# A decoder trunk on eight cores: four chunk loads issued by ScalarE, one norm weight moved, new durations in the scheduler's table

## The reference, cut to what matters

```python
def rmsnorm(x, g):
    return x * rsqrt(mean(x * x, -1) + EPS) * g

for layer in range(2):                      # x: (16, 2048, 1024) float32
    xn = rmsnorm(h, mix_norm_g[layer])
    if layer == 0:
        a, xb, gate_b, gate_c = split(xn @ ab_w_in)          # 4 x 512 columns
        a_out = (trailing mean of a over 2/4/8/16 positions - a) @ pool_w * pool_scale
        b_out = gate_b * conv3(gate_c * xb)                  # causal, width 3
        mix = concat(a_out, b_out) @ ab_w_out
    else:
        u, v, q, k, val = split(xn @ cd_w_in)
        c_out = gelu(u) * (W_s layernorm(gelu(v)) + b)       # chunks of 128 positions
        d_out = stick_breaking_attention(q, k, val)          # strictly causal, 8 heads
        mix = concat(c_out, d_out) @ cd_w_out
    h = h + mix
    h = h + square(relu(rmsnorm(h, mlp_norm_g[layer]) @ w1)) @ w2     # 1024 -> 4096 -> 1024
return rmsnorm(h, final_norm_g)
```

## Time and profile before

| | us |
|---|---|
| median of 3 runs | 2603.14 (2600.72 to 2603.9) |
| the profiled execution, its own time | 2602.82 |
| its slowest core, first to last instruction | 2601.3 (core 6); the other seven 2588.6 to 2600.9 |
| TensorE busy on core 6 | 2523.2 (97%) |
| VectorE, ScalarE, GpSimd busy | 1583.2, 1117.3, 658.0 |
| granted TensorE clock, mean | 0.992 on core 6, 0.991 to 0.994 on the others |
| chain that ended last | TensorE 91%, VectorE 3%, transfers 3%, issue 2%, ScalarE 1% |

### The profile page before, as it was taken

How to read it: one execution, slowest core, us unless ns; L and a number is a source line. 1 busy time by engine, 2 the same in 40 slices (tenths; PEclk the granted TensorE clock), 3 DMA queues, 4 the chain that set the end, 5 groups by cost and what they waited for, 6 DMA issues and landing times.

```text
span 2601.3 us, 38509 instructions; the slowest of 8 cores (2588.6 to 2601.3 us)
## 1 busy us (share of the span) xinstructions
PE 2523.2 (97%) x12055; PEld 1108.3 (43%) x12055; DVE 1583.2 (61%) x2344; ACT 1117.3 (43%) x1749; POOL 658.0 (25%) x1088
## 2 busy tenths in 40 slices
PE   6899999999999999999999999999999999999996
PEld 2344444444444444444444444444444444444342
DVE  4761338567586565457577533677666777767554
ACT  3335223464335643174333444345543465345432
POOL 4531111212112253611245211212212122112121
PEclk9999999999999999999999999999999999999998
DMA  9777885745446897887572233433444335435544
GB/s 186 148 139 153 175 183 132 179 98 131 120 124 153 152 181 155 213 264 231 176 210 84 70 104 104 132 102 86 123 121 134 98 90 118 117 97 165 181 146 144
DMA packets 216686, 371.81 MB, mean 143 GB/s; under 512 B 90208, under 2 KB 98016, under 8 KB 216480
## 3 DMA queue, kind: packets, MB, share of 16 engines
q0 software_dynamic: 79664, 238.86, 38.3%
q1 hardware_dynamic: 136240, 129.36, 16.9%
q10 hardware_dynamic: 576, 1.05, 0.1%
HBM read 308.62 MB, written 95.42 MB: 155 GB/s over the span
## 4 chain that ended last, share of the span: by engine, by line
PE 91%; DVE 3%; DMA 3%; issue 2%; ACT 1%; SPq 0%; POOL 0%; DVEq 0%; ACTq 0%; POOLq 0%
PE ps L1400 62%; PE ps L1524 20%; PE ps L1616 6%; DMA h<-xT 2%; PE ps L2283 1%; PE ps L2240 1%; DVE xn L1416 1%; DMA ring<-wcm 1%; DVE Y L1416 1%; SPq L1721 0%; ACT ps L1409 0%; PE ps L2101 0%; DVE h L1413 0%; DVE xn L1413 0%; DVE mix L1413 0%
## 5 line engine op out<-in xcount | busy, mean ns | idle before, releaser
L1400 PE MATMUL ps<-xn,ring 128*128 128x512 bf16 x4960 | 1113.5, 381 | 9.0 <-DVE mix L1413 5.3
L1413 DVE TENSOR_TENSOR h<-ps,h 128x512 f32<-128x512 f32 x816 | 553.3, 688 | 526.2 <-PE ps L1400 295.3
L1400 PEld LDWEIGHTS ps<-xn,ring 128*128 128x128 bf16 x4960 | 473.9, 98 | 578.1 <-issue 20.8
L1409 ACT ACTIVATE ps<-ps 128x512 f32<-128x512 f32 x644 | 375.0, 583 | 703.2 <-PE ps L1400 324.7
L1338 POOL DMA_DIRECT2D ring<-wcm x269 | 143.9, 536 | 779.9 <-PE ps L1400 268.0
L1524 PE MATMUL ps<-hid,ring 128*128 128x512 bf16 x1408 | 327.6, 380 | 2.6 <-DMA ring<-wcm 2.2
L1409 ACT ACTIVATE hid<-ps 128x512 bf16<-128x512 f32 x496 | 294.4, 598 | 37.0 <-ACT ps L1409 1.9
L1338 POOL DMA_DIRECT2D ring<-wsc x308 | 165.9, 539 | 487.7 <-PE ps L1400 189.4
L1409 ACT ACTIVATE xn<-h 128x2048 bf16<-128x2048 f32 (+1 forms) x98 | 154.0, 1591 | 311.9 <-DVE h L1413 291.8
L1400 PE MATMUL ps<-hid,ring 128*128 128x512 bf16 x1280 | 281.0, 380 | 0.0
L1524 PE MATMUL ps<-TT,ring 128*128 128x512 bf16 x1056 | 255.4, 381 | 3.8 <-ACT ps L1409 3.1
(11 more groups left out here) (123 smaller groups left out, 1694.2 us busy)
## 6 DMA issues: line engine op xcount, KB each, us to landing
ring<-wsc POOLq DMA_DIRECT2D x308, 256.0 KB, 3.1
ring<-wblk POOLq DMA_DIRECT2D x188, 256.0 KB, 5.6
ring<-wcm POOLq DMA_DIRECT2D x93, 512.0 KB, 4.0
ring<-wcm POOLq DMA_DIRECT2D x118, 384.0 KB, 4.0
wsc<-ring SPq DMA_DIRECT2D x116, 256.0 KB, 4.2
wcm<-TT SPq DMA_DIRECT2D x64, 256.0 KB, 2.8
oT<-stg SPq DMA_DIRECT2D x56, 256.0 KB, 5.8
wcm<-ring SPq DMA_DIRECT2D x52, 256.0 KB, 4.1
```

Of the source, the lines that this page charges most:

```text
L1400: ins = pe.matmul(out, lhsT=l, rhs=r, start=(i == 0), stop=(i == n - 1), **({"skip_group_check": True} if skip else {}))
L1409: return self.S.op("act", lambda e: e.activation(out=out, in_=in_, func=func, **kw), rd=rd, wr=wr, dur=0.17 + n * 0.00083, aset=aset)
L1413: return self.S.op(eng, lambda e: e.tensor_tensor(out=out, in0=a, in1=b, op=op), rd=rd, wr=wr, dur=dur)
```

## The change

Three kinds of edit. (1) Of the first tile's eight chunks of x, the odd ones are issued by ScalarE, the even ones by SyncE as before. (2) In the last tile the norm weight of chunk 7 is no longer applied by a ScalarE copy; VectorE multiplies h by weight and ms in one instruction. (3) Durations in the scheduler's table become longer: the sums of a norm, Ln and Exp (`act` adds 0.17 + n * 0.00083), the pooled evictions, the convolution, GpSimd's additions, the attention's first matmuls. A margin per operation is added; its two constants equal `MARGIN`, and the boost `PB` that one of them replaces is 0, so both are without effect.

```diff
+RMARG = 0.6
+PMARG = 0.6
...
-                    r = end if e == "pe" else (r if x.tight else r + MARGIN)
+                    r = end if e == "pe" else (r if x.tight else r + x.marg)
...
-                self.S.op("sp", (lambda t, c, src: (lambda e: e.dma_start(out=self.h[s][:, t, c:c + w, :], in_=src)))(t, c, src),
+                q = "act" if s == 0 and p == 0 and t == 0 and c % 2 else "sp"
+                self.S.op(q, (lambda t, c, src: (lambda e: e.dma_start(out=self.h[s][:, t, c:c + w, :], in_=src)))(t, c, src),
...
-            self.tt("dve", xn[:, t, 0:4, :], xn[:, t, 0:4, :], xn[:, t, 4:8, :], ALU.add, tx, tx[0:4], 1.22)
+            self.tt("dve", xn[:, t, 0:4, :], xn[:, t, 0:4, :], xn[:, t, 4:8, :], ALU.add, tx, tx[0:4], 1.29)
...
-            self.act(self.ms[m][:], self.bap(bi), AF.Ln, [self.t_bank[bi], self.t_cf], [self.t_ms[m]], 512, aset="ln",
+            self.act(self.ms[m][:], self.bap(bi), AF.Ln, [self.t_bank[bi], self.t_cf], [self.t_ms[m]], 620, aset="ln",
...
-                            self.tt("dve", h[:, t, c, :], h[:, t, c, :], self.ms[m][:], ALU.mult,
-                                    [th[c], self.t_ms[m]], [th[c]], 0.65)
+                            if c < 7:
+                                self.tt("dve", h[:, t, c, :], h[:, t, c, :], self.ms[m][:], ALU.mult,
+                                        [th[c], self.t_ms[m]], [th[c]], 0.65)
+                            else:
+                                self.stt(h[:, t, c, :], h[:, t, c, :], g, self.ms[m][:], ALU.mult, ALU.mult,
+                                         [th[c], self.t_ms[m], self.t_cf], [th[c]])
...
-                if final is not None:
+                if final is not None and c < 7:
...
-                         [self.t_Y], 0.15 + 1.15 * fw)
+                         [self.t_Y], 0.15 + 1.41 * fw)
...
-                            [td], 0.15 + 1.9 * fw)
+                            [td], 0.15 + 2.0 * fw)
...
-                S.op("pe", fz, rd=rk + [tm[t][4 + a]], wr=zt, dur=0.25, boost=ZB)
+                S.op("pe", fz, rd=rk + [tm[t][4 + a]], wr=zt, dur=0.28, boost=ZB)
```

More of the change, by code:

```diff
@@ L90 @@
     __slots__ = ("eng", "fn", "deps", "dma", "dur", "lat", "nbytes", "idx", "late", "start", "end",
-                 "sig", "chan", "val", "val2", "vc", "waits", "succ", "npend", "ready", "aset", "boost", "tight")
+                 "sig", "chan", "val", "val2", "vc", "waits", "succ", "npend", "ready", "aset", "boost", "tight", "marg")
 SEMLAT = 0.12
@@ L123, in op @@
         o.tight = False
+        o.marg = MARGIN
         o.eng = eng
@@ L1737, in sums @@
         def sums():
-            self.tt("dve", xn[:, t, 0:4, :], xn[:, t, 0:4, :], xn[:, t, 4:8, :], ALU.add, tx, tx[0:4], 1.22)
-            self.tt("dve", xn[:, t, 0:2, :], xn[:, t, 0:2, :], xn[:, t, 2:4, :], ALU.add, tx[0:4], tx[0:2], 0.69)
-            self.tt("dve", xn[:, t, 0, :], xn[:, t, 0, :], xn[:, t, 1, :], ALU.add, tx[0:2], tx[0:1], 0.43)
+            self.tt("dve", xn[:, t, 0:4, :], xn[:, t, 0:4, :], xn[:, t, 4:8, :], ALU.add, tx, tx[0:4], 1.29)
+            self.tt("dve", xn[:, t, 0:2, :], xn[:, t, 0:2, :], xn[:, t, 2:4, :], ALU.add, tx[0:4], tx[0:2], 0.74)
+            self.tt("dve", xn[:, t, 0, :], xn[:, t, 0, :], xn[:, t, 1, :], ALU.add, tx[0:2], tx[0:1], 0.52)
         def boosted(f, x):
@@ L1754, in rstd @@
                 o.boost = RB
+                o.marg = RMARG
         def rstd1():
@@ L1765, in rstd1 @@
             st["m"] = m
-            self.act(self.ms[m][:], self.bap(bi), AF.Ln, [self.t_bank[bi], self.t_cf], [self.t_ms[m]], 512, aset="ln",
+            self.act(self.ms[m][:], self.bap(bi), AF.Ln, [self.t_bank[bi], self.t_cf], [self.t_ms[m]], 620, aset="ln",
                      scale=1.0 / D, bias=self.cf[:, 60:61])
-            self.act(self.ms[m][:], self.ms[m][:], AF.Exp, [self.t_ms[m]], [self.t_ms[m]], 512, aset="ln", scale=-0.5)
+            self.act(self.ms[m][:], self.ms[m][:], AF.Exp, [self.t_ms[m]], [self.t_ms[m]], 555, aset="ln", scale=-0.5)
         def apply(c0, c1):
@@ L1831, in f @@
                     self.mms(self.bap(bi), [(self.cb[:, 128 + g * 128:256 + g * 128], pb[:, c:c + 512])],
-                             [self.t_cb, self.t_pb], [self.t_bank[bi]], 0.25).boost = PB
-                    self.act(mx[:, t, g, :], self.bap(bi), AF.Copy, [self.t_bank[bi], self.t_cf], [tm[t][g]], 512,
+                             [self.t_cb, self.t_pb], [self.t_bank[bi]], 0.25).marg = PMARG
+                    self.act(mx[:, t, g, :], self.bap(bi), AF.Copy, [self.t_bank[bi], self.t_cf], [tm[t][g]], 620,
                              scale=cf[:, 40 + g:41 + g])
@@ L1861, in f @@
                 b = cf[:, 56 + i:57 + i]
-                self.act(Y[:, 0:W], PR[:, 2:2 + W], AF.Identity, [self.t_PR, self.t_cf], [self.t_Y], W, scale=w2, bias=b)
+                self.act(Y[:, 0:W], PR[:, 2:2 + W], AF.Identity, [self.t_PR, self.t_cf], [self.t_Y], W * 1.26, scale=w2, bias=b)
                 self.stt(Y[:, 0:W], PR[:, 1:1 + W], w1, Y[:, 0:W], ALU.mult, ALU.add, [self.t_PR, self.t_Y, self.t_cf],
-                         [self.t_Y], 0.15 + 1.15 * fw)
+                         [self.t_Y], 0.15 + 1.41 * fw)
                 self.stt(Y[:, 0:W], PR[:, 0:W], w0, Y[:, 0:W], ALU.mult, ALU.add, [self.t_PR, self.t_Y, self.t_cf],
-                         [self.t_Y], 0.15 + 1.15 * fw)
+                         [self.t_Y], 0.15 + 1.41 * fw)
                 if more:
```

## The result

The changed kernel takes 2610.76 us (median of 11 runs, 2606.52 to 3081.85) against 2603.14 (11 runs, 2598.34 to 2950.49). Ratio of the comparable runs: **1.0023, 95% interval 1.0014 to 1.0032**, some 6 us slower. The time lies in the range on record (2597 to 2611), at its upper end. The likeliest case (2604) was not what happened; the slower rival (2610.3) was.

A forecast was written before the change was run, and what follows sets the result against it. TensorE, busy 2523.2 of 2601.3 us, was taken to bound the kernel, so only its 78 us of standing and the clock could change. Terms summed to +1.15 on 2602.8, giving 2604.0 us; 8-in-10 range 2597 to 2611.

The forecast's parts named there:

- likeliest case: Whole kernel: about 2604 us, own range 2599 to 2608; together with no change, within 5.2 us, chance 0.54.
- slower rival: First projection: the early square's transfer lands 2 us later, other gains halved; +7.5, 2610.3 us, chance 0.24.
- largest term: 52 to 97 us: evictions queue behind a square waiting for its transfer, delaying VectorE; +4.5 us, from 3.1 and 6.1.
- VectorE's products beginning 2.4 us later: First projection: four more evictions ahead of Ln delay the norm products from 69.05 to 71.4 us.
- TensorE's own wait absorbed: First projection: TensorE's new 5-us wait is offset as the waits before 75.14, 79.10 and 96.28 shrink, 5.5 together.
- The price of the half clock: After TensorE's wait near 78.67 us on core 3: the lower clock takes 3.4 us of multiplying away.
- One of the two additions surely meets products: First projection: moved GpSimd additions slow VectorE's norm products, up to 2 * 1.5 = +3.0 us; the middle was taken.
- The head: Start of the kernel: split issue lands the first tile sooner; −0.7 us, bounds −3.0 to +0.5.
- if two queues fill the idle share: 2 to 7 us: a second issuing queue uses 2.1 us of unused DMA time, landing the tile 2.1 us sooner.
- faster rival: Start and first projection: transfers 2 to 3 us earlier, small stall, small gains whole; −7.5, 2595.3 us, chance 0.22.
- the gains elsewhere: At 186, 1387, and 784 with 2057 us: releasers of TensorE's waits move earlier; −0.5, −0.4 and −1.3 us.
- the attention's row: Attention, 1700 to 2070 us: some residual additions move behind a scan; +0.8 us, bounds 0 to +3.0.

The follow-up runs named there:

- e3: Kernel before with one ScalarE square (h1, second tile, first half), and another standing between, moved ahead of a PA eviction: ratio 1.0014, mean of core spans +3.7 us.
- e4: Changed kernel with that one square put back behind two PA evictions and one XB eviction: ratio 1.0004 to the kernel before.
- e1: Kernel before with only the split issue of the first tile's chunks: ratio 1.0001, mean of core spans −0.2 us.
- e7: Kernel before with some forty short queue stretches reordered, plus the split issue: ratio 1.0000, mean of core spans −4.9 us.
- e8: Kernel before with only the hand-reordered queue stretches before 200 us: ratio 1.0000, mean of core spans −2.1 us, 58 to 130 us −3.7.
- e10: Kernel before with three GpSimd additions cut to 48 columns, no square moved: ratio 0.9988, mean of core spans +0.1 us.
- e2: Kernel before with only the new durations table, issue and norm weight as before: ratio 1.0031, mean of core spans +6.1 us.

## Why the prediction was right or wrong

**Right: the place and the cause.** The wait of over 8 us for h<-xT, PA's evictions behind it, TensorE's wait of up to 5.6 us ending at 61 to 67 us and the lower clock all stand in the profile, and e3 and e4 show that the square brings them.

**Right in sum, not term by term: the size.** The largest term (+4.5 for the first projection, −1.0 behind it) came out at +4.9 and −1.9. But it was built on VectorE's products beginning 2.4 us later, with TensorE's own wait absorbed. They did not begin later: at 66.6 us before and 66.7 in the change, mean of the cores, since the square itself started earlier (62.8 and 61.0). And TensorE's wait was not absorbed: of the 4.0 us that 58 to 72 us grew, 72 to 90 gave back 2.0. The rest of the +4.9 is 90 to 110 us, where the wait before the last pb is 3.66 on every core, and e4 shows that this one is not the square's. That the sum fits is in part luck: from core to core the same term runs from +0.9 to +8.3, and it was worked out on one core. The price of the half clock, 3.4, was too high as well: in that window TensorE worked 5.33 us on 13 matmuls, which take 2.8 at 0.22 each, so it took 2.5 away.

**Right: the norm weight.** From the end of the last square to the start of Ln there were 0.90 us before, with the copy between (the first row below, core 6, to 2580.06), and 0.61 after (the other two, core 3): 0.3 for a forecast of 0.25. The whole is too small for the runs to show.

```profile
2578.53 0.63 ACT L1409 ACTIVATE xn<-h 128x512 bf16<-128x512 f32 x1 [0.50 <-DVE h L1413]
```
```profile
2581.77 0.63 ACT L1412 ACTIVATE xn<-h 128x512 bf16<-128x512 f32 x1 [0.22 <-DVE h L1416]
2583.01 0.69 ACT L1412 ACTIVATE ms<-ps,cfs 128x512 f32<-128x512 f32 x1 [0.62 <-PE ps L1409]
```

**Half right: the contention.** "One of the two additions surely meets products": two did. The first four products took 6.18 us, 3.2 more than 4 × 0.75. But the term booked this as a new cost, and it is an old one in another place. Before, the same additions stood beside the three sums, which took 5.74 us; in the change the sums run free of them. The last two on core 3, against 2.22 and 2.10 us before:

```profile
53.71 0.69 DVE L1416 TENSOR_TENSOR xn<-xn 128x1024 bf16<-128x1024 bf16 x1
...
54.51 0.42 DVE L1416 TENSOR_TENSOR xn<-xn 128x512 bf16<-128x512 bf16 x1
```

So some 3.2 us were saved on the sums and 3.2 paid on the products, and VectorE's busy time on the page grew by only 2.0 us in all. The 5.5 us that the prediction let the later waits absorb were a sum of core 6's; on cores with shorter waits there is less to absorb.

**The head: the number met by chance.** −0.7 was taken and −0.7 measured in one pair of profiles, but that mean has an error of 0.7, e3 is 1.6 shorter there without the split, e1 gives −0.2 in the whole and e7 no gain. The step "if two queues fill the idle share" was the wrong reading: a busy share of 0.58 was no free 0.42. The faster rival rested on it and falls.

**Wrong: the gains elsewhere.** −0.5, −0.4 and −1.3 at 186, 1387, 784 and 2057 became +0.5, +0.3 and +0.4 (the last for 784; 2057 lies in the attention's row). The step that failed is that of reading a wait as won when its releaser moves up. At 186 us the waits of 1.90 and 0.41 did go, and 1.42 for pb and 1.40 for hid took their place, which the prediction named and valued too low. With these terms at their measured values (+1.2 instead of −2.2) the sum would have been 4.6, not 1.15, and 2607.4 us.

**Not foreseen: the waits for transfers** further on (+2.0 in one pair of profiles). Part of it may be chance: cores differ there by up to 6 us either way. But the queues are not the same there. The traces of before and after show other orders on VectorE from 800 to 1000 us and near 1100 and 2100, and on SyncE, which issues transfers, from 850 to 950 and 1100 to 1200. The prediction has no term for these moves, and no run separates them from chance. e8 shows something of the kind the other way round: what was won early was partly missing at the end.

The forecast of "no change" thus rested on small gains that offset a loss whose sum was right. The price of the rival (+7.5) was near the truth, though by other terms: no later landing was needed.

## What to carry to other kernels

In an in-order queue an instruction that waits for a transfer is a lock on everything behind it. Before a durations table is changed, look at what its new order puts behind such instructions; here one square ahead of two evictions cost 3.7 us. Compare each new entry with the trace, too: here some came nearer to it and some went away from it. When a wait is removed, count the next two releasers before booking a gain, and book small gains that depend on an order at zero. When an instruction moves beside one that slows it, ask what that one slowed before. Replaying the queues with durations and transfer times taken from the trace, and moving only around the waits that it shows, gave 0.5%.

## What the runs showed of the hardware

- Three bf16 sums on VectorE took 5.74 us while GpSimd added in float32, and 2.58 when its additions were short. Norm products took 6.04 us for four beside additions and 2.74 without (both e4, core 3, below). This is a far larger cost than any entry that the table changed. What it costs the whole kernel is not shown: e10 took it off three sums and became no faster that its runs can tell (0.9988, 0.9965 to 1.0012).
- The DMA engines' busy share in 2 to 7 us was 0.83 (mean of the cores) with two issuing queues in e1 and 0.69 with one in e2, and the tile's last chunk landed at 15.3 and 15.5 us. With one queue in e3 it was 0.78 and 14.3.

```profile
63.58 2.74 DVE L1427 SCALAR_TENSOR_TENSOR xn<-h,cfs,ms 128x512 bf16<-128x512 f32 x4 [5.58 <-ACT ms L1420]
...
76.55 6.04 DVE L1427 SCALAR_TENSOR_TENSOR xn<-h,cfs,ms 128x512 bf16<-128x512 f32 x4
```
